# State-space stage of a decoder trunk: the first quarter's decays inside the convolution loop, and the outputs added up ahead of the next decays

## What is computed

```
proj = h @ w_in;  z, xbc, dt = split(proj)          # 2048, 2560 and 32 columns
xbc  = silu(causal_depthwise_conv(xbc, w, b));  xs, bm, cm = split(xbc)
dt   = softplus(dt + dt_bias);  a = -exp(a_log)
# scan, in 2 chunks of 128 tokens, 32 heads of 64
a_cs      = cumsum(dt * a)                          # in each chunk
decay_in  = exp(where(tril, a_cs[l] - a_cs[s], -inf))
cb        = C[l] . B[s]                             # per group of 16 heads
y_diag    = (cb * decay_in) @ (x * dt)
state     = B^T @ (decay_out * x * dt)              # of chunk 0, used by chunk 1
y_off     = exp(a_cs) * (C @ state)
y = y_diag + y_off + d * x
g = rmsnorm_per_group(y * silu(z)) * norm_w;  out = g @ w_out
```

## Time and profile before

| | us |
|---|---|
| median of 3 runs | 1380.33 (1377.47 to 1383.94) |
| the profiled execution | 1380.16 |
| its span in the trace | 1378.3 |
| TensorE busy | 1326.3 (96%) |
| VectorE busy | 855.8 (62%) |
| ScalarE busy | 665.1 (48%) |
| state-space stage, about | 655 to 850 of the span |

### The profile page before, as it was taken

How to read it: one execution, slowest core, us unless ns; L and a number is a source line. 1 busy time by engine, 2 the same in 40 slices (tenths; PEclk the granted TensorE clock), 3 DMA queues, 4 the chain that set the end, 5 groups by cost and what they waited for, 6 DMA issues and landing times.

```text
span 1378.3 us, 20308 instructions
## 1 busy us (share of the span) xinstructions
PE 1326.3 (96%) x8604; PEld 1212.2 (88%) x8604; DVE 855.8 (62%) x1125; ACT 665.1 (48%) x834; POOL 40.6 (3%) x59
## 2 busy tenths in 40 slices
PE   5899999999999999998997999999999999999997
PEld 5788899999899899997997988999988898899996
DVE  4777765554655665555898786655556676665553
ACT  4455454444455444443765554544444555544442
POOL 2000000000000000000101110000000000000000
PEclk9899999999999999999999999999998999999999
DMA  8644276555654475543773444755535133475540
GB/s 254 161 126 150 95 239 203 187 188 177 169 168 153 169 245 183 184 157 97 246 229 108 142 156 136 239 190 193 194 92 203 54 133 124 168 244 184 184 153 31
DMA packets 147834, 231.06 MB, mean 168 GB/s; under 512 B 7651, under 2 KB 116493, under 8 KB 147744
## 3 DMA queue, kind: packets, MB, share of 16 engines
q1 hardware_dynamic: 144896, 221.66, 48.7%
q0 software_dynamic: 2848, 8.10, 2.7%
HBM read 227.08 MB, written 2.65 MB: 167 GB/s over the span
## 4 chain that ended last, share of the span: by engine, by line
PE 86%; DVE 7%; ACT 3%; DMA 2%; issue 1%; POOL 0%; SPq 0%; DVEq 0%; POOLq 0%; ACTq 0%
PE bank L511 15%; PE bank L513 14%; PE bank L512 14%; PE acc L717 11%; PE acc L716 11%; PE acc L720 11%; PE bank L857 3%; DVE wlo L494 3%; ACT whi L484 1%; PE bank L903 1%; PE bank L640 1%; DMA raw<-in_mla_w_in 1%; DMA raw<-in_mla_w_ukv 1%; PE bank L884 1%; PE bank L1377 1%
## 5 line engine op out<-in xcount | busy, mean ns | idle before, releaser
L494 DVE TENSOR_TENSOR wlo<-raw,whi 128x2048 fp32r<-128x2048 f32 (+1 forms) x209 | 467.8, 2245 | 188.0 <-ACT whi L484 187.9
L484 ACT ACTIVATE whi<-raw 128x2048 fp32r<-128x2048 f32 (+1 forms) x209 | 389.2, 1871 | 91.8 <-PE acc L720 79.2
L511 PE MATMUL bank<-hhi,whi 128*128 128x256 f32 x1448 | 414.7, 286 | 6.4 <-DVE xn L1647 4.0
L513 PE MATMUL bank<-hhi,wlo 128*128 128x256 f32 x1448 | 410.9, 284 | 0.0
L512 PE MATMUL bank<-hlo,whi 128*128 128x256 f32 x1448 | 410.9, 284 | 0.0
L511 PEld LDWEIGHTS bank<-hhi,whi 128*128 128x128 f32 x1448 | 278.1, 192 | 12.5 <-issue 8.2
L512 PEld LDWEIGHTS bank<-hlo,whi 128*128 128x128 f32 x1448 | 278.0, 192 | 3.4 <-issue 1.0
L513 PEld LDWEIGHTS bank<-hhi,wlo 128*128 128x128 f32 x1448 | 277.9, 192 | 0.2
L717 PE MATMUL acc<-wlo,uhi 128*128 128x512 f32 x512 | 200.0, 391 | 0.0
L716 PE MATMUL acc<-whi,uhi 128*128 128x512 f32 x512 | 199.6, 390 | 0.0
L720 PE MATMUL acc<-whi,ulo 128*128 128x512 f32 x512 | 159.2, 389 | 0.0
(11 more groups left out here) (213 smaller groups left out, 1673.2 us busy)
## 6 DMA issues: line engine op xcount, KB each, us to landing
raw<-in_mlp_w SPq DMA_DIRECT2D x128, 1024.0 KB, 5.3
raw<-in_ssd_w_in SPq DMA_DIRECT2D x18, 1024.0 KB, 6.0
raw<-in_mla_w_o SPq DMA_DIRECT2D x16, 1024.0 KB, 4.8
raw<-in_mla_w_ukv SPq DMA_DIRECT2D x8, 1024.0 KB, 6.3
raw<-in_moba_w_qkv SPq DMA_DIRECT2D x16, 512.0 KB, 7.4
raw<-in_ssd_w_out SPq DMA_DIRECT2D x8, 1024.0 KB, 4.9
raw<-in_mla_w_uq SPq DMA_DIRECT2D x8, 768.0 KB, 8.3
raw<-in_mla_w_in SPq DMA_DIRECT2D x4, 1024.0 KB, 8.1
```

The lines of the kernel that those rows point to most:

```text
L484: nc.scalar.activation(whi[:, s, :e], raw[:, s, :e], ACT.Copy).then_inc(w_hi_done[s], 1)
L494: nc.vector.tensor_tensor(wlo[:, s, :e], raw[:, s, :e], whi[:, s, :e].bitcast(F32), ALU.subtract).then_inc(w_split[s], 1)
L511: nc.tensor.matmul(ps, lhs[0], rhs[0], start=start, stop=False)
L513: return nc.tensor.matmul(ps, lhs[1], rhs[0], start=False, stop=stop)
```

## The change

Two things. (1) The work on the first quarter's decays moves from the start of the scan into the convolution loop: DVE does `diffs(0)` after block 5 and both `decay_cb(0, c)` after block 8 (with the wait for `cbm`, which stood behind the loop), and ACT does `decays(0)` after the silu of block 6, in the round of block 7. (2) In quarters 0 to 2 DVE's `diffs(q + 1)` moves from ahead of the two steps of `y_sb` to behind them, and the split of a weight unit that stood last moves ahead of `decay_cb(q + 1, c)`. No instruction is added or taken away, and TensorE's, POOL's and SP's programs stay.

```diff
--- before.py
+++ after.py
@@ -1448,6 +1448,12 @@
             job_copied(act, "scol")
             dst = [BT, CT] + [xsT[:, 2 * n:2 * n + 2, :] for n in range(ZT // 2)]
 
+            def decays(q):
+                for c in range(T):
+                    b = (2 * q + c) % 4
+                    act.wait_ge(dec_diff, 2 * q + c + 1)
+                    nc.scalar.activation(dec[:, b], dec[:, b], ACT.Exp).then_inc(dec_exp, 1)
+
             def silu(n):
                 act.wait_ge(conv_done, n + 1)
                 nc.scalar.activation(dst[n][:] if n < 2 else dst[n], cacc[:, n % 2], ACT.Silu).then_inc(silu_done, 1)
@@ -1477,14 +1483,10 @@
                     ps = job_ready(act, "Btok")
                     nc.scalar.activation(Btok[:].rearrange("p a b -> p (a b)"), ps[:, 0:SSD_G * P],
                                          ACT.Copy).then_inc(freed("Btok"), 1)
+                if n == 7:
+                    decays(0)
             silu(9)
             act.wait_ge(silu_done, 10)
-
-            def decays(q):
-                for c in range(T):
-                    b = (2 * q + c) % 4
-                    act.wait_ge(dec_diff, 2 * q + c + 1)
-                    nc.scalar.activation(dec[:, b], dec[:, b], ACT.Exp).then_inc(dec_exp, 1)
 
             def gate_square(n):
 
@@ -1501,7 +1503,6 @@
                                                scale=scol[:, 100 + 2 * n + i:101 + 2 * n + i])
                 ins.then_inc(ghi_done, 1)
 
-            decays(0)
             for q in range(5):
                 if 0 < q < 4:
                     for n in (2 * q - 2, 2 * q - 1):
@@ -1607,7 +1608,13 @@
                     ps = job_ready(dve, "cb")
                     nc.vector.tensor_tensor(cbm[:].rearrange("p g c l -> p (g c) l"), ps[:].rearrange("p (a l) -> p a l", a=4),
                                             upper[:].unsqueeze(1).to_broadcast([P, 4, P]), ALU.mult).then_inc(freed("cb"), 1)
-            job_copied(dve, "cb")
+                if n == 5:
+                    diffs(0)
+                if n == 8:
+                    job_copied(dve, "cb")
+                    decay_cb(0, 0)
+                    decay_cb(0, 1)
+
             def gate(n):
 
                 ps = job_ready(dve, ("yT", n // 2, n % 2))
@@ -1657,10 +1664,6 @@
                                             xdt[:, 0, :].rearrange("p (h d) -> p h d", h=8),
                                             tokv[:, 4, hs].unsqueeze(2).to_broadcast([P, 8, SSD_HD]),
                                             ALU.mult).then_inc(dx_done, 1)
-                if q == 0:
-                    diffs(0)
-                    decay_cb(0, 0)
-                    decay_cb(0, 1)
                 if q == 4:
                     dve_splits(dve, ("so", L, 4))
                 if q:
@@ -1682,8 +1685,6 @@
                 if q < 4:
                     dve_splits(dve, ("z", 2 * q), AHEAD - 1)
                     dve_splits(dve, ("z", 2 * q + 1), AHEAD - 1)
-                    if q < 3:
-                        diffs(q + 1)
                     ps = job_ready(dve, ("yo", q))
                     nc.vector.tensor_tensor(y_sb[:, 1, :].rearrange("p (h d) -> p h d", h=8),
                                             ps[:].rearrange("p (h d) -> p h d", h=8),
@@ -1693,9 +1694,11 @@
                     ps = job_ready(dve, ("yd", q, 1))
                     nc.vector.tensor_tensor(y_sb[:, 1, :], ps[:], y_sb[:, 1, :], ALU.add).then_inc(freed(("yd", q, 1)), 1)
                     if q < 3:
+                        diffs(q + 1)
+                    dve_splits(dve, ("z", 2 * q + 1))
+                    if q < 3:
                         decay_cb(q + 1, 0)
                         decay_cb(q + 1, 1)
-                    dve_splits(dve, ("z", 2 * q + 1))
                 if q == 2:
                     mean_square(0)
                 if q == 4:
```

## The result

| | before | changed |
|---|---|---|
| median, 18 runs each | 1381.40 us | 1384.59 us |
| lowest to highest | 1377.47 to 1385.24 | 1383.14 to 1388.01 |
| span of the profiled execution | 1378.3 us | 1383.2 us |
| ratio to before, 95% interval | | 1.0021 (1.0012 to 1.0031) |

What follows compares the result with a forecast made beforehand. DVE was taken to bound the kernel from the convolution's end to `("z", 2)`, TensorE behind it. 1380.16 us profiled + 3.0 schedule + 1.7 clock = 1384.9 us, 0.34% slower; range 1379.3 to 1389.3.

Steps and rivals of the forecast that it cites:

- What bounds: State-space stage: DVE is the bound from the convolution's end to `("z", 2)` at 748.16; behind it TensorE sets the pace.
- The loop: Convolution loop: 5.4 us added, 2.5 of slack used, 1.0 lost waiting for `whi`; DVE leaves 3.6 us later.
- The new wait: Quarter 0, ahead of the state product `st`: TensorE waits 3.3 us for `dxdt`, from 727.4 to 730.7.
- Part 2: Quarters' reordering: the 3.1 us hole ahead of the output transposes closes; TensorE idles 7.3 us in one piece before `("z", 2)`.
- whole schedule term: Start of `("z", 2)`: 751.15 where it was 748.16, so the schedule costs 3.0 us.
- The clock: `("z", 1)`, behind the new pause: 3.5 us at half clock, 1.7 us lost; bounds 0 and 3.4.
- first pause: TensorE's new 3.3 us pause ahead of `st`, expected to drop the clock to half for 3.5 us.
- second recovery: Cold restart at `("z", 2)`, 3.35 us before; could last 3.4 us longer, to 1.7 us more; 0 more taken.
- (a): New pause ahead of `st`: same schedule but no clock drop, 1383.2 us; chance 0.17.
- (b): Convolution loop has more slack and hides the decays; `("z", 2)` starts 0.3 us earlier, 1379.9 us; chance 0.13.
- (c): New pause drops the clock 6.8 us, long pause delays second recovery: 8.1 us, 1388.3; chance 0.15 together with (d).
- (d): Loop: `decay_cb(0, c)` or `diffs(0)` find inputs late; time that of (c); chance nearly nothing, 0.15 together with (c).

Runs made afterwards that it cites:

- Experiment 4: Changed kernel with quarter 0's two `cbm` products moved from round 8 of the loop to behind `dxdt`; median 1381.90 us, ratio to before 1.0002.
- experiment 2: Kernel before with only the change's new order in the quarters, quarter 0's decays staying behind the loop; median 1383.05 us, ratio 0.9998.
- experiment 3: Idle matmuls put into TensorE's pauses: kernel before 1377.65 us, changed kernel 1382.35 us, changed kernel with only its first pause filled 1383.29 us (medians).
- the loop part alone: Changed kernel with the quarters' order put back, `diffs(q + 1)` ahead of the `y_sb` steps again; median 1382.98 us, ratio to before 1.0009.
- the filled kernel before: Kernel before with 22 and 30 idle matmuls in TensorE's two pauses between quarters 0 and 1; medians 1377.65 and 1378.23 us in two runs.

## Why the prediction was right

**What bounds.** DVE up to `("z", 2)`, TensorE behind it: borne out. What was lost by quarter 1's state product is there unchanged at the stage's end: the two timelines are 5.96 us apart at both places (755.44 and 761.40; 848.53 and 854.49).

**The loop.** From the start of quarter 0's differences in round 6 to the end of block 9's taps the forecast had 25.76 us (702.97 to 728.73); the trace has 25.80 (703.82 to 729.62). The wait for `whi` in round 8, put at 1.0, is 0.99. The stretch, forecast from 702.97, starts 0.85 later in this execution, as the transposes of `xsT` do.

**The new wait.** 3.3 us forecast, 3.16 measured, and the state product is 3.32 us later (9.94 against 6.62 us behind the transposes). Experiment 4 shows that it is the loop's load.

**Part 2.** The closed wait for `y_sb` and a pause of 7.3 us: 7.19 measured, and neutral by itself (experiment 2). The whole schedule term, 3.0, measures 2.92 and 2.95 with the clock held up (experiment 3). DVE's idling ahead of the next `xdt`, 2.56 and 3.38 in rows 8, was to shrink by 1.6 to 1.8 and has done so:

```profile
784.07 1.29 DVE L1654 TENSOR_TENSOR xn<-bank,tokv 128x512 f32<-128x512 f32 x2 [0.91 <-PE bank L1399]
814.41 0.69 DVE L1654 TENSOR_TENSOR xn<-bank,tokv 128x512 f32<-128x512 f32 x1 [1.73 <-PE bank L1399]
```

**The clock** is the term that was mis-sized, in both directions. In the profile the drop behind the first pause lasted 3.4 us, where I had assumed 3.5, and cost 1.42 us instead of 1.7. The second recovery, for which I took nothing extra, lasted 5.1 us behind the restart instead of 3.35 and cost 0.75 more. All in all 2.20 us against 1.7. In the whole times it was less: 2.9 us (1.7 to 4.3) in all leaves about nothing beside the schedule's 2.9, and the 4.7 that I forecast lie outside that interval. No experiment shows what in the rest of the kernel makes up for the 2.20 us. The forecast of the difference is right for the profiled executions, which are 4.80 us apart (1384.96 - 1380.16). That 1384.9 met the median 1384.59 is largely luck: the medians of before moved up by 1.1 us between 3 and 18 runs, and the forecast stood on the lower one, so that a difference put too high met a start that was too low.

**The rivals.** (a), no drop, with 3.0 us, fits the measured 2.9 better than the forecast's 4.7 does, but not the profiles, both of which (of the changed kernel) show the drop. (b), a loop that hides the decays, falls by the wait of 3.16 us. (c) never occurred whole, but both of its parts did: the drop of 6.8 us behind the first pause in the loop part alone, the longer second recovery in the changed kernel. So its chance was not idle. (d) did not happen. In the loop the exponential starts 1.29 us after its table load, and the loop's length came out on that price. The drain of about 1380 ns that the Trainium skill adds (ScalarE: Activation LUTs, What ACT_TABLE_LOAD costs) is not to be seen here either. The 0.6 us by which the forecast let that drain delay DVE is too small by its own chain: DVE already stands waiting for the `whi` behind the exponentials, so 1.4 us more on ACT would move DVE's exit by 1.4, an estimate from that page's figure.

```profile
712.55 1.28 ACT L1455 ACT_TABLE_LOAD   x1
713.84 2.01 ACT L1455 ACTIVATE dec<-dec 128x1024 f32<-128x1024 f32 x2
```

## What to carry to other kernels

Look at where an engine has its gaps before moving work: a loop with 0.84 us of slack in each of three rounds can't hide 5.4 us, and the gaps that the work leaves behind (DVE's 4.6 and 4.1 us) are then of no use. When an engine is what another waits for, order its work by who needs it next: in the changed kernel freeing a bank (0.6 us of work that TensorE wanted at once) stood behind 7.6 us of differences, split and `cbm` products, and TensorE did not need the last of these for another 14. Freeing the bank first gained 4.7 us over before by itself and 8.7 us with the differences in the loop. Closing a wait earns nothing if the work that it hid now stands in front of the next one.

## What was not expected

A pause costs more than its length. The same pauses of the same kernel, filled with idle matmuls, made the stage 1.43 us shorter before and 3.63 us shorter in the changed kernel, and the two medians of the filled kernel before were 4 us under it, of which 1.43 us are traced to these pauses. After a pause of 3.16 to 3.18 us the clock was at half for 3.4 us in two profiles and for 6.8 in another, and after single pauses of 7.2 us for 6.8 to 10.2 us; so one profile prices a pause only to about 2 us (an estimate: 3.4 us more at half clock, with TensorE busy, are 1.7 us).
